# Up rows of four selections stacked on the partitions, summed in four column strips of TensorE

## What is computed

```python
u = expert_down[experts]          # 16 rows of 1024 per token and head
vv = expert_up[experts]
act = gelu(einsum("thkd,td->thk", u, hb))
y = einsum("thk,thkd->td", gates * act, vv)   # summed over the heads too
return x + gate2 * y
```

## Time and profile before

| | |
|---|---|
| median of 3 runs | 3002.66 us (3001.5 to 3003.53) |
| the profiled execution | 2994.11 us, of which the span of the trace is 2992.3 us |
| first gather issued | 1497.4 us |
| late work ends | about 2140 us |
| PE, DVE, ACT, POOL busy over the span | 88%, 55%, 27%, 39% |
| gathers | 1024, 536.94 MB |

### The profile page before, as it was taken

One profiled execution on the slowest core, in us unless ns is written; L12 is line 12 of the kernel. 1 busy time (PEld: TensorE's weight loads), 2 busy tenths in 40 slices (PEclk: granted clock), 3 DMA queues, 4 the chain that ended last, 5 costly groups with the idle time before them and its releaser, 6 DMA issues.

```text
span 2992.3 us, 26054 instructions
## 1 busy us (share of the span) xinstructions
PE 2625.3 (88%) x8398; PEld 1372.6 (46%) x8398; DVE 1659.1 (55%) x3647; ACT 795.6 (27%) x1616; POOL 1169.9 (39%) x1091
## 2 busy tenths in 40 slices
PE   7999899999979979989799899979877778767777
PEld 3444444445544436467675465546422223223232
DVE  2056823345510124364379998765677777777764
ACT  2013312138730012232234323221312112212121
POOL 0000000013310000000057777656777777777776
PEclk8999999999989989999899899989999899989999
DMA  7226103122221113321379989999999999999998
GB/s 307 74 113 274 64 30 112 57 85 71 65 91 56 57 64 133 127 85 57 109 257 357 354 305 379 380 351 344 357 376 395 400 408 405 405 405 405 406 402 354
DMA packets 185462, 709.01 MB, mean 237 GB/s; under 512 B 20416, under 2 KB 43344, under 8 KB 175216
## 3 DMA queue, kind: packets, MB, share of 16 engines
q0 software_dynamic: 147456, 536.94, 46.7%
q1 hardware_dynamic: 37584, 169.45, 15.2%
q10 hardware_dynamic: 288, 0.96, 0.1%
HBM read 703.01 MB, written 4.27 MB: 236 GB/s over the span
## 4 chain that ended last, share of the span: by engine, by line
PE 22%; POOL 14%; issue 7%; DMA 5%; DVE 3%; ACT 0%; POOLq 0%; SPq 0%; DVEq 0%; ACTq 0%
PE bank L3193 14%; POOL ring L3001 11%; PE bank L488 4%; DMA ring<-in_peer_expert_down,experts 3%; POOL second_arena L3001 3%; DVE ring L3076 1%; PE bank L2035 0%; DMA second_arena<-in_peer_expert_down,experts 0%; DMA ring<-in_peer_expert_up,experts 0%; DMA x_rows_scratch<-second_arena 0%; DMA out<-xT 0%; PE bank L2012 0%; PE bank L2329 0%; PE bank L2336 0%; PE bank L2334 0%
## 5 line engine op out<-in xcount | busy, mean ns | idle before, releaser
L3193 PE MATMUL bank<-ring,xT 128*128 128x512 f32 x1516 | 765.6, 643 | 189.0 <-ACT xT L3169 81.4
L3076 DVE CUSTOM_DVE_ANT_0 ring<-ring,second_arena 128x1024 f32<-128x1024 f32 x380 | 465.9, 1226 | 219.8 <-DMA ring<-in_peer_expert_down,experts 172.4
L3193 PEld LDWEIGHTS bank<-ring,xT 128*128 128x128 f32 x1516 | 292.2, 203 | 600.4 <-issue 376.3
L3001 POOL DMA_INDIRECT ring<-in_peer_expert_up,experts x384 | 412.5, 1074 | 159.0 <-issue 96.7
L3001 POOL DMA_INDIRECT ring<-in_peer_expert_down,experts x380 | 402.4, 1059 | 131.3 <-issue 114.3
L488 PE MATMUL bank<-hT,ring 128*128 128x512 f32 (+2 forms) x1168 | 433.2, 530 | 6.4 <-DMA ring<-in_weights 1.8
L488 PEld LDWEIGHTS bank<-hT,ring 128*128 128x128 f32 (+1 forms) x1168 | 222.3, 193 | 211.0 <-issue 199.8
L1420 POOL TENSOR_TENSOR xs_skip<-xs_rows,rows 128x512 f32<-128x512 f32 x16 | 24.7, 1546 | 727.4 <-ACT xs_rows L1298 638.3
L3001 POOL DMA_INDIRECT second_arena<-in_peer_expert_down,experts x132 | 137.0, 1038 | 434.9 <-DVE experts L3059 390.6
L3169 ACT ACTIVATE xT<-consts,expert_coefs 128x128 f32<-128x128 f32 x505 | 177.9, 394 | 414.4 <-PE bank L3193 278.5
L3193 PE MATMUL bank<-second_arena,xT 128*128 128x512 f32 x504 | 239.2, 607 | 22.5 <-DMA second_arena<-in_peer_expert_up,experts 22.4
(11 more groups left out here) (527 smaller groups left out, 3107.7 us busy)
## 6 DMA issues: line engine op xcount, KB each, us to landing
ring<-in_weights SPq DMA_DIRECT2D x65, 2048.0 KB, 8.1
second_arena<-in_weights SPq DMA_DIRECT2D x12, 1024.0 KB, 8.2
decay<-acum_scratch SPq DMA_DIRECT2D x16, 512.0 KB, 5.2
ring<-in_peer_expert_up,experts POOLq DMA_INDIRECT x384, 7.3
ring<-in_peer_expert_down,experts POOLq DMA_INDIRECT x380, 7.1
second_arena<-in_peer_expert_down,experts POOLq DMA_INDIRECT x132, 6.5
x_rows<-in_x SPq DMA_DIRECT2D x1, 2048.0 KB, 12.0
x_rows_scratch<-second_arena SPq DMA_DIRECT2D x2, 1024.0 KB, 8.7
```

The source lines that it names most:

```text
L3001: pool.indirect_dma_start(out=slot[seat[n]], out_offset=None, in_=d[f"peer_expert_{kind}_2"], in_offset=bass.IndirectOffsetOnAxis(ap=exper ...
L3076: post(dve, dve.tensor_tensor_reduce(row, row, h_row(i), 1.0, 0.0, ALU.mult, ALU.add, dots[:, u % 2, s:s + 1]), dotted)
L3193: last = pe.matmul(k.bank[half][:], diag[n % DR], row[:, half * 512:(half + 1) * 512], start=(h == 0 and s == 0), stop=(h == RH - 1 and s ...
```

## The change

Up gathers no longer bring one selection for 128 tokens. One gather brings four selections for 32 tokens: gather `4j + g` of a unit carries on partitions 32s to 32s+31 the rows that tokens 32g to 32g+31 chose as selection 4j + s. The indices for this are stacked by ACT (`stack`) into a new tensor `up_rows`, and the coefficients into `up_coef`, by 16 small copies each per unit. POOL waits for the stacked indices (`stacked`) before the first up gather of a unit. The stationary operand becomes 128x32: four identities of 32x32 stacked, scaled by the stacked coefficients. The matmul writes 32 partitions of the bank, so four gathers fill the four strips of a bank. PE takes the up rows in groups of four: it waits for four gathers and four operands, and then issues eight matmuls. There are 16 operand buffers in place of eight. The share of the last unit that DVE summed is gone.

```diff
-    DR = 8
+    DR = 16
+    SW = 32
...
+        up_coef = spent[:, 2, 0:2 * RK].rearrange("p (a s) -> p a s", a=2)
+        strip_ident = spent[:, 2, 64:64 + SW]
...
+                if kind == "up" and s == 0:
+                    pool.wait_ge(stacked.sem, u + 1)
...
+                which = experts[:, i, j:j + 1] if kind == "down" else t.up_rows[:, u % 4, s:s + 1]
...
-            sum_apart()
...
+            def stack(out, rows):
+                out = out.rearrange("p (q s) -> p s q", s=4)
+                for s in range(4):
+                    for j in range(4):
+                        last = act.activation(out[j * SW:(j + 1) * SW, s, :], rows[s * SW:(s + 1) * SW, 4 * j:4 * j + 4],
+                                              ACT.Copy)
+                return last
...
+                act.wait_ge(routed.sem, u + 1)
+                if u >= 4:
+
+                    act.wait_ge(summed, (u - 3) * RK)
+                post(act, stack(t.up_rows[:, u % 4, :], experts[:, i, h * RK:(h + 1) * RK]), stacked)
...
+                post(act, stack(up_coef[:, u % 2, :], coef[:, u % 2, :]), k.astep)
...
-                        act.activation(diag[n % DR], k.const("ident"), ACT.Copy,
-                                       scale=coef[:, u % 2, s:s + 1]).then_inc(diag_ok.sem, 1)
+                    act.activation(diag[n % DR], strip_ident, ACT.Copy,
+                                   scale=up_coef[:, u % 2, s:s + 1]).then_inc(diag_ok.sem, 1)
...
-                for s in range(RK):
-                    other.upto(RK * (u + 1) + s + 2)
+                for q in range(RK // 4):
+                    n = RK * u + 4 * q
+                    other.upto(RK * (u + 1) + 4 * q + 2)
...
-                    row = arrived(pe, ("up", u, s))
-                    pe.wait_ge(diag_ok.sem, n + 1)
+                    rows = [arrived(pe, ("up", u, 4 * q + s)) for s in range(4)]
+                    pe.wait_ge(diag_ok.sem, n + 4)
                     for half in range(2):
-                        last = pe.matmul(k.bank[half][:], diag[n % DR], row[:, half * 512:(half + 1) * 512],
-                                         start=(h == 0 and s == 0), stop=(h == RH - 1 and s == RK - 1))
-                    last.then_inc(summed, 1)
+                        for s in range(4):
+                            last = pe.matmul(k.bank[half][s * SW:(s + 1) * SW, :], diag[(n + s) % DR],
+                                             rows[s][:, half * 512:(half + 1) * 512],
+                                             start=(h == 0 and q == 0), stop=(h == RH - 1 and q == RK // 4 - 1))
+                            if half == 1:
+                                last.then_inc(summed, 1)
```

More of the change, by code:

```diff
@@ L2929, in expert_stage @@
         spent = k.xT[:, :, 0:H2]
-        diag = [spent[:, n // 2, (n % 2) * P:(n % 2 + 1) * P] for n in range(DR)]
+        diag = [spent[:, n // 8, (n % 8) * SW:(n % 8 + 1) * SW] for n in range(DR)]
+        up_coef = spent[:, 2, 0:2 * RK].rearrange("p (a s) -> p a s", a=2)
+        strip_ident = spent[:, 2, 64:64 + SW]
         x_back = spent[:, 4:8, :]
@@ L2942, in expert_stage @@
         weighed = Signal(ctx, nc, "expert_coefs_ready")
+        stacked = Signal(ctx, nc, "up_experts_stacked")
         diag_ok = Signal(ctx, nc, "coef_diagonal_ready")
@@ L2958, in scores @@
             return halves[i // HT].scores[i % HT]
[L2960 to L2964, removed]
         def finish_tick(i):
@@ L3091, in weigh @@
                                                    ALU.mult, ALU.mult), weighed)
-            def sum_apart():
-                u = N - 1
-                for s in range(RK):
[L3097 to L3106, removed]
             def finish(i):
-                dve.wait_ge(summed, (i + 1) * NSEL - (apart if i == NT - 1 else 0))
+                dve.wait_ge(summed, (i + 1) * NSEL)
                 for half in range(2):
@@ L3162, in _ @@
                 act.wait_ge(weighed.sem, u + 1)
+                if u == 0:
+                    for s in range(4):
+                        at = slice(s * SW, (s + 1) * SW)
+                        act.activation(strip_ident[at, :], k.const("ident")[at, at], ACT.Copy)
+                post(act, stack(up_coef[:, u % 2, :], coef[:, u % 2, :]), k.astep)
                 for s in range(RK):
                     n = diag_ok.n
-                    if not by_vector(u, s):
-                        if n >= DR:
-                            act.wait_ge(summed, n - DR + 1)
-                        act.activation(diag[n % DR], k.const("ident"), ACT.Copy,
-                                       scale=coef[:, u % 2, s:s + 1]).then_inc(diag_ok.sem, 1)
-                        diag_ok.n += 1
+                    if n >= DR:
+                        act.wait_ge(summed, n - DR + 1)
+                    act.activation(diag[n % DR], strip_ident, ACT.Copy,
+                                   scale=up_coef[:, u % 2, s:s + 1]).then_inc(diag_ok.sem, 1)
+                    diag_ok.n += 1
                     if s + 1 < RK:
@@ L3179, in _ @@
             other = Woven(chain(late, "tensor", pe, left_stage))
-            n = -1
             for u, (i, h) in enumerate(units):
-                for s in range(RK):
-                    other.upto(RK * (u + 1) + s + 2)
[L3184 to L3187, removed]
+                for q in range(RK // 4):
+                    n = RK * u + 4 * q
+                    other.upto(RK * (u + 1) + 4 * q + 2)
+                    if i > 0 and h == 0 and q == 0:
                         pe.wait_ge(written.sem, i)
-                    row = arrived(pe, ("up", u, s))
-                    pe.wait_ge(diag_ok.sem, n + 1)
+                    rows = [arrived(pe, ("up", u, 4 * q + s)) for s in range(4)]
+                    pe.wait_ge(diag_ok.sem, n + 4)
                     for half in range(2):
-                        last = pe.matmul(k.bank[half][:], diag[n % DR], row[:, half * 512:(half + 1) * 512],
-                                         start=(h == 0 and s == 0), stop=(h == RH - 1 and s == RK - 1))
-                    last.then_inc(summed, 1)
+                        for s in range(4):
+                            last = pe.matmul(k.bank[half][s * SW:(s + 1) * SW, :], diag[(n + s) % DR],
[3 more added lines that the diff above has]
+                                last.then_inc(summed, 1)
         @block.sync
@@ L3223, in second_block @@
         t.dots, t.coef = sb("expert_dots", [P, 2, RK]), sb("expert_coefs", [P, 2, RK])
+        t.up_rows = sb("stacked_experts", [P, 4, RK], I32)
         t.left = sb("scores_left_over", [P, RK * RK])
```

2 lines of the change are left out of this document (1 added, 1 removed).

## The result

The changed kernel takes 2980.40 us (median of 15 runs, 2968.10 to 2997.22), the kernel before 3000.13 us in the same rounds (15 runs, 2988.04 to 3012.41). The ratio is 0.9939, 95% interval 0.9921 to 0.9957: 0.6% faster. The profiled execution took 2980.20 us with a span of 2978.4, 13.9 us less than the one of before. Executions of one kernel lie up to 1% apart here, so two traces can differ by several us with no cause in the change. The first gather alone is issued anywhere from 1495.9 to 1507.8 us in the traces of this document, also where the edit acts only later.

The account below looks back on a forecast made before the run. The prediction took PE as the bound in 2000:2120 and the DMA engines from 2400 on. A gain of 24 us less 4 us for ACT gave 20 us less: median 2982.7 us, 0.67% faster, eight-in-ten range 2956 to 3010.

Parts of the forecast that it names:

- The cost of a group: On PE, four up rows were to cost 1.85 to 3.64 us instead of 6.8 us.
- The gain, 24 us: POOL's true waits for PE that go away, 16.7 us of them in 2000:2120; bounds 0 and 56 us.
- the last rival: Long stalls behind DVE and SP shrink too, 16 to 20 us more gained, about 2960 us; chance 0.11.
- the first rival: Gathers are bound by POOL and DVE, not PE; POOL's issues lengthen, about 2999 us; chance 0.17.
- ACT's copies, 4 us: Late work queued on ACT behind the copies, charged 0.4 us for each of some 11 units; bounds 0 and 33.
- Held slots, nothing: Up slots freed only when their group is done come back within the 13.0 us allowed, so cost nothing.
- Moved ticks, nothing: PE's late ticks in one burst behind a group cost nothing; upper bound 2.0 us of delay at the lower clock.
- the rival of stalled DVE: Bursts of late work on PE stall DVE, 1 us for each of 46 groups, about 3028 us; chance 0.14.
- The end, nothing: At the program's end the last group finishes between 0.5 us earlier and 1.2 us later, taken as 0.
- The limit of about 358 GB/s: HBM limit by which 2000:2120 could shrink only 7.4 us and the sum be 15; set aside for the trace's 405.

Follow-up runs that it names:

- E6: The changed kernel without any of ACT's stacking copies, so rows and factors are wrong: 2961.82 us, ratio 0.9877 to the kernel before.
- E5: The changed kernel again, nothing edited, as a reference: 2978.41 us, ratio 0.9929 to the kernel before.
- E3: The kernel before with 32 unused copies of 32x4 a unit added on ACT: 3115.52 us, ratio 1.0051 to the kernel before.
- E2: The kernel before with PE waiting for four rows and four diagonals, late work in bursts, matmuls whole: 3189.83 us, ratio 1.0295 to the kernel before.
- E7: The changed kernel with PE taking two late ticks before each half of a group's columns: 3010.09 us, ratio 1.0033 to the kernel before.
- E8: The changed kernel with all late ticks due by a group's fourth row run before the group: 3037.87 us, ratio 1.0126 to the kernel before.
- E9: The changed kernel without the 16 index-stacking copies a unit, coefficients still stacked: 3089.78 us, ratio 0.9983 to the kernel before.
- E1: The kernel before with each up matmul taking 128 of its 512 columns: 3073.90 us, ratio 0.9911 to the kernel before.

## Why the prediction came true

It gave 2982.7 us and 0.67% faster; measured were 2980.4 us and 0.61%. The direction is right, and so is the mechanism of the gain. The size is right by luck: two terms, each too small by 13 us, cancel.

- **The cost of a group**, 1.85 to 3.64 us, is what the trace shows: 1.92 us (records overlap by 0.07) and 3.64 us.
- **The gain, 24 us, was mis-sized.** E6 has all of it without the stacking, and stands 1 - 0.9877 = 1.2%, 37 us, below the kernel before. The table splits it, as far as single traces go. POOL's stand over all gathers is 84.2 us before and 59.1 in E6, 25 us less, so the 24 us of waiting for PE were counted about right. 16.2 of them lie in gathers 288 to 383, where 16.7 were counted, and 10.0 in 128 to 287, where only 2.3 and part of 2 were: the long stalls shrank in part, as the last rival had it at chance 0.11. The term that was missing is POOL's issues: in all they fell by 12 us, 96 x (1.166 - 1.038) = 12.3 of it in 288 to 383. No term had them shorter, and the first rival had them grow. Down gathers into the ring average 1.008 us in 2000:2120 of the changed kernel, where they took 1.307; why their overlap with the dots changed, no run shows.
- **ACT's copies, 4 us, were mis-sized.** The durations were good: 0.207 us, begun 0.218 us apart (estimate 0.19), 0.234 us for an operand (0.24). What failed is the charge of 0.4 us a unit for what stands behind them. E5 and E6 differ by 16.6 us, 1.5 us for each of 11 units. It lies inside the bounds given, 0 to 33, and E3 has 13 to 16 us for the same copies in the kernel before. In the two traces of the changed kernel POOL's stand is only 7 and 11 us less than before, and not 20; the shorter issues, 10 and 14 us, make up the rest. The step "behind the coefficients" named the right place, since PE's first group waits there (ten of the 18 waits for operands before 2140 are of a unit's first group, 58.7 of 76.8 us), but priced only the late work queued on ACT and not PE, whose rows then hold POOL's slots.
- **Held slots, nothing.** From 2400 POOL's idle time ended by PE is 4.1 us in 11 waits, 0.8 net of 0.30 us each, against 1.1. The limit of 13 us itself was not tested: E2 frees its slots row by row.
- **Moved ticks, nothing.** DVE's waits for PE in 1500:2140 add up to 22.6 us, from 53.8 before, so the rival of stalled DVE did not occur. That a cheaper PE would also serve DVE sooner was in no term. E7 and E8 moved ticks the other way, two or three earlier, which cost 1 to 2% through POOL's slots.
- **The end, nothing.** The last gather is issued at 2961.3 and PE ends at 2972.0, 10.7 us later; before, 2975.8 and 2986.0, 10.2 us. That is 0.5 us more.
- **The limit of about 358 GB/s** that the Trainium skill gives (DMA: Bandwidth & Descriptors, Specifications) does not hold for this core: 408 GB/s in 2000:2120, where by it only 7.4 us were to be had.

Open are the split of the 16.6 us between the two stackings, why POOL's issues became shorter, and how the change does on the slower chips.

## What to carry to other kernels

When a change makes one engine cheap and adds small work to an idle one, ask who waits behind that work in the unit's first step. Here 7 us of copies a unit, on an engine that is busy a third of the time, cost 1.5 us a unit, and PE stood 29 us more with its rows there. A wait is put down to what came last, and it can hide another that ended just before: compare it with the landing of the rows before you price it. Consumption in groups cost nothing that could be seen where the consumer had time to spare (E6, and E2 after the late work), and 3% where it had next to none (E2 before 2140 us). And a forecast that comes true should be taken apart as well as a failed one, since here 24 - 4 and 37 - 17 give the same 20.

## What the runs showed of the hardware

The chips differ in what the gathers get. From 2400 on in the changed kernel the DMA moves 401 GB/s, with few dips. On the slower chips (5, 8 and 11) the same stretch gives 360 to 366 GB/s in all eight kernels; GB/s in 40 slices of 2400:2960 in E9:

```profile
GB/s 385 356 399 364 369 326 383 353 411 323 363 388 368 361 389 301 328 384 408 331 317 357 375 372 380 326 399 410 386 307 353 382 372 358 410 271 347 376 374 354
```

Single slices of 14 us reach 411 GB/s, as on the faster chips, and others fall to 271. So it looks like interruptions and not a lower ceiling; no row names their source.

Where PE became cheaper its granted clock was lower: over 2400:2800 it is 0.93 before, with PE busy 306 of 400 us, and 0.63 in the changed kernel, with 136. On chip 5 it is 0.88 in E3, with 277 us, and 0.51 in E1, with 158. The group of 1.92 us ran at a granted clock of 1.00 (2.4 GHz) and the one of 3.64 us at 0.50 (1.2 GHz). POOL's true wait for PE after 2400 stayed at 0.8 us all the same. E1's stretch:

```profile
2400.00:2800.00 400.00, 158.08 (x550) 124.32 (x550) 260.25 (x627) 71.19 (x167) 292.05 (x272) 0.51 0.95 360
```
